# Three of eight samples' recurrent states moved from the attention heads into the last items of the in-projection

## The reference

```python
def step(h, inp):
    x_t, dt_t, da_t, b_t, c_t = inp
    h = jnp.exp(da_t)[..., None, None] * h + jnp.einsum('bgjp,bgn->bgjpn', x_t * dt_t[..., None], b_t)
    return h, jnp.einsum('bgjpn,bgn->bgjp', h, c_t)
```

## Time and profile before

| | |
|---|---|
| median of 3 runs | 593.87 us (593.57 to 593.93) |
| the profiled execution | 591.05 us, its span 589.3 us |
| busy in the span: PE, PEld, DVE, ACT, POOL | 531.9 (90%), 449.1 (76%), 384.9 (65%), 290.6 (49%), 77.7 (13%) us |
| 0 to 130 us: PE, DVE, ACT busy | 117.59, 91.11, 44.72 us |
| 130 to 313 us (items with page steps) | 181.53, 101.81, 89.02 us |
| 313 to 348 us (bridge) | 33.92, 21.23, 22.78 us |
| 470 to 481 us (end of the heads) | 0.22, 10.73, 2.52 us |
| 481 to 589.3 us (out-projection and tail) | 96.93, 77.97, 45.94 us |

### The profile page before, as it was taken

One profiled execution on the slowest core, in us unless ns is written; L12 is line 12 of the kernel. 1 busy time (PEld: TensorE's weight loads), 2 busy tenths in 40 slices (PEclk: granted clock), 3 DMA queues, 4 the chain that ended last, 5 costly groups with the idle time before them and its releaser, 6 DMA issues.

```text
span 589.3 us, 12342 instructions
## 1 busy us (share of the span) xinstructions
PE 531.9 (90%) x4726; PEld 449.1 (76%) x4726; DVE 384.9 (65%) x735; ACT 290.6 (49%) x624; POOL 77.7 (13%) x102
## 2 busy tenths in 40 slices
PE   4999998999999999999998999898787639999992
PEld 4899997998888888888885456566543339999992
DVE  5674987766555677445334753767677898795675
ACT  7333232143565554552614754877858645645320
POOL 2110000000000000000002412433431000210520
PEclk9999999999999999999999999888989959999997
DMA  8233032296889877788753342432470083669552
GB/s 333 108 143 97 30 97 86 71 315 222 255 268 283 265 256 250 239 309 289 246 191 97 93 133 82 110 81 60 148 256 19 6 303 115 223 202 367 188 157 72
DMA packets 55692, 104.12 MB, mean 177 GB/s; under 512 B 7193, under 2 KB 25986, under 8 KB 55378
## 3 DMA queue, kind: packets, MB, share of 16 engines
q1 hardware_dynamic: 55634, 103.33, 53.7%
HBM read 95.68 MB, written 7.73 MB: 175 GB/s over the span
## 4 chain that ended last, share of the span: by engine, by line
PE 76%; DVE 14%; ACT 6%; issue 3%; DMA 1%; POOL 0%; DVEq 0%; SPq 0%; ACTq 0%
PE pm L1488 18%; PE pm L1490 16%; PE pm L1489 16%; PE px L1571 4%; PE px L1587 3%; PE px L1760 3%; PE px L1758 3%; PE pm L1709 2%; ACT dec L723 1%; PE pm L1747 1%; DVE hring L1175 1%; PE px L1700 1%; PE px L1723 1%; DVE w_lo L880 1%; DVE xbc L1239 1%
## 5 line engine op out<-in xcount | busy, mean ns | idle before, releaser
L1488 PE MATMUL pm<-xw_hi,w_lo 128*128 128x260 f32 x544 | 162.3, 298 | 9.4 <-DVE w_lo L1007 8.3
L1489 PE MATMUL pm<-xw_lo,w_hi 128*128 128x260 f32 x544 | 154.4, 284 | 0.0
L1490 PE MATMUL pm<-xw_hi,w_hi 128*128 128x260 f32 x544 | 154.2, 283 | 0.0
L1488 PEld LDWEIGHTS pm<-xw_hi,w_lo 128*128 128x128 f32 x544 | 103.0, 189 | 24.6 <-issue 11.9
L553 ACT ACTIVATE w_hi<-w_raw 128x1024 fp32r<-128x1024 f32 (+1 forms) x70 | 72.0, 1035 | 83.0 <-PE pm L1490 76.7
L880 DVE TENSOR_TENSOR w_lo<-w_raw,w_hi 128x1024 fp32r<-128x1024 f32 (+1 forms) x70 | 85.9, 1236 | 29.0 <-ACT w_hi L553 29.0
L1489 PEld LDWEIGHTS pm<-xw_lo,w_hi 128*128 128x128 f32 x544 | 103.1, 190 | 0.2
L1490 PEld LDWEIGHTS pm<-xw_hi,w_hi 128*128 128x128 f32 x544 | 103.1, 189 | 0.0
L1488 PE MATMUL pm<-mix_hi,w_lo 128*128 128x260 f32 x256 | 73.7, 288 | 11.8 <-DVE mixlo_s L1233 11.3
L1490 PE MATMUL pm<-mix_hi,w_hi 128*128 128x260 f32 x256 | 73.2, 286 | 0.0
L1488 PEld LDWEIGHTS pm<-mix_hi,w_lo 128*128 128x128 f32 x256 | 49.2, 192 | 12.4 <-issue 12.1
(11 more groups left out here) (273 smaller groups left out, 1048.7 us busy)
## 6 DMA issues: line engine op xcount, KB each, us to landing
page<-in_cache SPq DMA_DIRECT2D x128, 288.0 KB, 3.6
w_raw<-in_w_in SPq DMA_DIRECT2D x34, 512.0 KB, 5.0
w_raw<-in_w_out SPq DMA_DIRECT2D x32, 512.0 KB, 4.7
dec<-ac_dram SPq DMA_DIRECT2D x16, 256.0 KB, 9.1
hring<-in_ssm_state SPq DMA_DIRECT2D x8, 512.0 KB, 6.5
o_ssms<-hring SPq DMA_DIRECT2D x8, 512.0 KB, 7.0
w_raw<-in_w_qb SPq DMA_DIRECT2D x6, 384.0 KB, 3.0
xraw<-in_xT SPq DMA_DIRECT2D x4, 520.0 KB, 6.4
```

Source lines behind the costliest of these rows:

```text
L1488: pe.matmul(out, wl, xh, start=start, stop=False)
L1489: pe.matmul(out, wh, xl, start=False, stop=False)
L1490: return pe.matmul(out, wh, xh, start=False, stop=stop)
```

## The change

Samples 0, 1 and 2 (quads 0 to 5) are updated and read out in items 33 to 38 (`EARLY_QUAD`), one quad at the end of each item on VectorE, by a new `early_dots` that takes the product in two pairs of rows, not one of four, since its scratch `prod_e` is half as wide. Their decays on ScalarE stand at the end of items 24, 25, 26, 27, 33 and 34 (`EARLY_DECAY`). Quads 6 to 9 take the places that are left in slots 5, 6 and 7; slots 1 to 4 hold none; the out-projection's quads stay.

For this, states 0 and 1 lie in the tiles of gates z 12 to 15, and VectorE waits for their stores before it evacuates items 36 and 38; state 2 lies where `u` is, and VectorE waits for its store before `state(2)` in the bridge. The samples' convolution moves from item 34 to item 27 and its SiLUs from item 36 to item 28. dxs is loaded in item 20 into `dxs_e` and its exponential taken in item 22, behind that item's SiLUs. The transpose, copy and store of B and C move to items 31 and 32. B and C of one group of one sample are broadcast for each early quad into one buffer `bc_e`, after the quad before is done. `dxs` and `ys` are copied at the end of the in-projection. SP's order follows: the loads of states 0 to 2, dxs, the conv state and the early broadcasts and stores stand among the weight and page loads, and the waits for early stores ahead of the first out-projection weights are gone.

```diff
+BC_STEP = [n for n in range(NSTEP) if SLOT[n][0] == 31][0] - 1
...
-SLOT_QUADS = {1: {3: 0}, 2: {3: 1}, 3: {3: 2}, 4: {3: 3}, 5: {3: 4, 4: 5}, 6: {3: 6, 4: 7}, 7: {1: 8, 3: 9}}
+NEARLY = 3
+EARLY_QUAD, EARLY_DECAY = {33 + n: n for n in range(2 * NEARLY)}, {24: 0, 25: 1, 26: 2, 27: 3, 33: 4, 34: 5}
+SLOT_QUADS = {5: {3: 6, 4: 7}, 6: {3: 8}, 7: {1: 9}}
...
-    hring = ([at("hring0", [P, 8, NS], F, G_ + 32768), at("hring1", [P, 8, NS], F, G_ + 20480)]
-             + [at(f"hring{b}", [P, 8, NS], F, A_ + 4096 * (b - 2)) for b in range(2, NB)])
+    hring = ([at(f"hring{b}", [P, 8, NS], F, off) for b, off in enumerate((B_ + 12 * TB, B_ + 14 * TB, H_ + TB))]
+             + [at(f"hring{b}", [P, 8, NS], F, A_ + 4096 * (b - NEARLY)) for b in range(NEARLY, NB)])
+    dxs_e = at("dxs_e", [P, 2, 8, NB], F, H_ + 3 * TB + 1024)
+    ys_e = at("ys_e", [P, 8, NEARLY], F, H_ + 3 * TB + 1536)
+    bc_t = at("bc_t", [32, P], F, H_ + 4 * TB + 1024)
+    prod_e = at("prod_e", [P, 2, NS], F, H_ + 4 * TB + 1024)
+    bc_e = at("bc_e", [P, 2, NS], F, H_ + 5 * TB + 1024)
...
-    stS = at("stS", [P, XT, 3, NB], F, H_ + TB)
+    stS = at("stS", [P, XT, 3, NB], F, B_ + 8 * TB)
...
+        def load_bc_e(n):
+
+            b, g = n // 2, n % 2
+            if n:
+                sp.wait_ge(v_dot, 4 * n)
+            sp.dma_start(bc_e, bc_dram.rearrange("(k g b) n -> b g k n", g=GR, b=NB)[b, g].partition_broadcast(P))\
+              .then_inc(s_bce, 16)
+
+        def store_early(b):
+            if b:
+                sp.wait_ge(s_hs0, 16 * b)
+            sp.wait_ge(v_h, 8 * b + 8)
+            sp.dma_start(a["o_ssms"][b], hring[b]).then_inc(s_hs0, 16)
...
-            if i == 31:
-                sp.wait_ge(a_silu, XT)
-                sp.dma_start(stS, a["conv_state"]).then_inc(s_sts, 16)
...
+            if i == 20:
+                sp.wait_ge(v_aux, X_QL)
+                sp.dma_start(stS, a["conv_state"]).then_inc(s_sts, 16)
+                sp.wait_ge(s_dsd, 16)
+                load_dxs()
+            if i in (21, 23):
+                load_state((i - 21) // 2)
+            if i == 32:
+                sp.wait_ge(a_silu, XT)
+                load_state(2)
+                sp.wait_ge(a_bct, 1)
+                sp.dma_start(bc_dram, bc_t).then_inc(s_bcd, 16)
+                sp.wait_ge(s_bcd, 16)
+            if i in EARLY_QUAD:
+                load_bc_e(EARLY_QUAD[i])
+            if i in (35, 37):
+                store_early((i - 35) // 2)
...
-        sp.wait_ge(s_dsd, 16)
-        load_dxs()
+        store_early(2)
...
-        sp.wait_ge(a_bct, 1)
-        sp.dma_start(bc_dram, u[1][0:32, 0:P]).then_inc(s_bcd, 16)
+        sp.wait_ge(p_pv, 2)
+        sp.wait_ge(v_dot, 8 * NEARLY)
...
-        load_state(0)
-        sp.wait_ge(p_st, 2 * NCH)
-        load_state(1)
-        sp.wait_ge(s_bcd, 16)
         sp.wait_ge(p_cb, 2)
-        load_bcs(0)
-        load_bcs(1)
+        load_bcs(3)
+        load_bcs(4)
...
-        load_state(2)
-        sp.wait_ge(s_ssm, 16)
-        for b in range(3, NB):
+        for b in range(NEARLY, NB):
             load_state(b)
-        load_bcs(2)
-        store_state(0)
-        store_state(1)
-        sp.wait_ge(s_hs0, 32)
-        sp.wait_ge(v_dot, 16)
...
-        load_bcs(3)
...
-        load_bcs(4)
         load_bcs(5)
...
             if i >= NIN + 20:
-                store_state(i - NIN - 18)
+                if i - NIN - 17 < NB:
+                    store_state(i - NIN - 17)
...
+        def state_decay(n, steps_):
+
+            b = n // 2
+            act.wait_ge(a_dx, 1)
+            act.wait_ge(s_hl[b], 16)
+            for t in range(4 * (n % 2), 4 * (n % 2) + 4):
+                act.activation(hring[b][:, t, :], hring[b][:, t, :], ACT.Copy, scale=steps_[:, 1, t, b:b + 1]).then_inc(a_h, 1)
...
+            if n == BC_STEP:
+                act.wait_ge(p_bct, 1)
+                act.activation(bc_t, px[0:32, 2, KVR:KVR + P], ACT.Copy).then_inc(a_bct, 1)
...
@@ -707,11 +742,16 @@
             if i in (ZT[7] + 1, ZT[11] + 1):
                 for t in range(4, 8) if i == ZT[7] + 1 else range(8, 12):
                     silu_z(t)
-                if i == ZT[11] + 1:
-                    act.wait_ge(v_cs, 1)
-                    act.wait_ge(g_last, XT)
-                    act.activation(xbc[:, 0:8, NT:TT], cvs[:, 0, 0:8], ACT.Silu).then_inc(a_cvs, 1)
-                    act.activation(cvs[:, 1], cvs[:, 0], ACT.Silu).then_inc(a_cvs, 1)
+            if i == 22:
+                act.wait_ge(s_dx, 64)
+                act.activation(dxs_e[:, 1], dxs_e[:, 1], ACT.Exp).then_inc(a_dx, 1)
+            if i == 28:
+                act.wait_ge(v_cs, 1)
+                act.wait_ge(g_last, XT)
+                act.activation(xbc[:, 0:8, NT:TT], cvs[:, 0, 0:8], ACT.Silu).then_inc(a_cvs, 1)
+                act.activation(cvs[:, 1], cvs[:, 0], ACT.Silu).then_inc(a_cvs, 1)
+            if i in EARLY_DECAY:
+                state_decay(EARLY_DECAY[i], dxs_e)
...
-        act.wait_ge(p_bct, 1)
-        act.activation(u[1][0:32, 0:P], px[0:32, 3, 0:P], ACT.Copy).then_inc(a_bct, 1)
...
-        act.wait_ge(s_dx, 64)
-        act.activation(dxs[:, 1], dxs[:, 1], ACT.Exp).then_inc(a_dx, 1)
...
+            if i in (ZT[12], ZT[14]):
+                dve.wait_ge(s_hs0, 16 if i == ZT[12] else 32)
...
+        def early_dots(n):
+
+            b, g = n // 2, n % 2
+            if n == 0:
+                dve.wait_ge(v_dx, 1)
+            dve.wait_ge(s_bce, 16 * (n + 1))
+            dve.wait_ge(a_h, 4 * n + 4)
+            for t in range(4 * g, 4 * g + 4):
+                dve.scalar_tensor_tensor(hring[b][:, t, :], bc_e[:, 0, :], dxs_e[:, 0, t, b:b + 1], hring[b][:, t, :],
+                                         ALU.mult, ALU.add).then_inc(v_h, 1)
+            dve.wait_ge(v_h, 4 * n + 4)
+            for k in range(2):
+                ts = slice(4 * g + 2 * k, 4 * g + 2 * k + 2)
+                if n or k:
+                    dve.wait_ge(v_dot, 4 * n + 2 * k)
+                link(dve.tensor_tensor(prod_e, hring[b][:, ts, :], bc_e[:, 1:2, :].to_broadcast([P, 2, NS]), ALU.mult))
+                dve.tensor_reduce(ys_e[:, ts, b:b + 1], prod_e, AX.X, ALU.add).then_inc(v_dot, 2)
...
-            if i == ZT[11] - 1:
+            if i == 27:
                 sample_conv()
+            if i == 29:
+                dve.wait_ge(a_cvs, 2)
+                dve.wait_ge(a_dx, 1)
+                dve.tensor_tensor(dxs_e[:, 0], xbc[:, 0:8, NT:TT], dxs_e[:, 0], ALU.mult).then_inc(v_dx, 1)
+            if i in EARLY_QUAD:
+                early_dots(EARLY_QUAD[i])
         sample_sum(NSTEP - 1)
         sample_out_t(1)
+        dve.tensor_copy(dxs, dxs_e).then_inc(v_dx, 1)
+        dve.tensor_copy(ys[:, :, 0:NEARLY], ys_e).then_inc(v_dx, 1)
...
+            if n == 2:
+                dve.wait_ge(s_hs0, 16 * NEARLY)
...
-            if n == 0:
-                dve.wait_ge(v_dx, 1)
-            dve.wait_ge(s_bcs[b % 2], 16 * (b // 2 + 1))
+            if n == 2 * NEARLY:
+                dve.wait_ge(v_dx, 3)
+            dve.wait_ge(s_bcs[b % 2], 16 * ((b - NEARLY) // 2 + 1))
...
-        dve.wait_ge(a_cvs, 2)
-        dve.wait_ge(a_dx, 1)
-        dve.tensor_tensor(dxs[:, 0], xbc[:, 0:8, NT:TT], dxs[:, 0], ALU.mult).then_inc(v_dx, 1)
...
+            if n == BC_STEP:
+                pe.wait_ge(a_cvs, 2)
+                pe.transpose(px[0:32, 2, KVR:KVR + P], cvs[:, 1, 8:12, :], cm[:, M_ID, :]).then_inc(p_bct, 1)
...
-        pe.wait_ge(a_cvs, 2)
         pe.wait_ge(v_cb, 2)
-        pe.transpose(px[0:32, 3, 0:P], cvs[:, 1, 8:12, :], cm[:, M_ID, :]).then_inc(p_bct, 1)
```

More of the change, by code:

```diff
@@ L726, in decays @@
             act.activation(dec[h % 6], dec[h % 6], ACT.Exp, scale=-1.0).then_inc(a_dec, 1)
-        def state_decay(n):
-            b = n // 2
-            act.wait_ge(s_hl[b], 16)
-            for t in range(4 * (n % 2), 4 * (n % 2) + 4):
-                act.activation(hring[b][:, t, :], hring[b][:, t, :], ACT.Copy, scale=dxs[:, 1, t, b:b + 1]).then_inc(a_h, 1)
         def gated_square(t):
@@ L830, in _ @@
                 for n in quads(s + 1, b):
-                    state_decay(n)
+                    state_decay(n, dxs)
             if 1 <= s <= 4:
```

30 lines of the change are left out of this document (13 added, 17 removed).

## The result

The changed kernel is slower: 604.70 us median of 4 runs (598.91 to 606.74) against 593.72 beside it on the same chip, ratio 1.018 (95% 1.013 to 1.022). The forecast was 591.5, its range ended at 596. The profiled execution took 605.37 us, its span (first instruction to last) is 603.3.

The account below looks back on a forecast made before the run. Four stages with different limits: TensorE nearly gapless except in the heads, where ScalarE's decays, then VectorE set the time. Gains of 8.8 us, less 5.5 in the in-projection and 1.0 in the bridge, gave -2.3: 591.5 us, range 587.5 to 596.

Parts of the forecast that it names:

- (d): In-projection, items 33 to 38: early quads wait for broadcasts landing in 4.9 us; costs 1.5 us, bounds 0 and 6.
- Rival 2: Early broadcasts land as slowly as the heads' bcs or worse, each early quad holding VectorE: 599 us; chance 0.12.
- SP's order: In-projection: dxs loads and the bc_dram wait ahead of weight and page loads cost 0, these being issued early enough.
- (a): In-projection, item 22: dxs exponential's table load comes ahead of ScalarE's copy of the probabilities; TensorE stands 0.8 us.
- (b): In-projection, items 24 and 26: ScalarE's state decays delay its copy of the probabilities, 0.5 us each, 1.0 together.
- (c): In-projection, item 27: sample_conv on VectorE delays the page sum, without slack; TensorE stands 2.2 us.
- The bridge: VectorE's third state step waits for the store of state 2, taken to land in 5.8 us; late by 1.0 us.
- The heads: Fewer quads on VectorE in the heads save 8.8 us: 2.1 and 1.6 at head 4, 5.1 in heads 6 and 7.
- Head 4's quad: Its removal moves the gate earlier, gain 2.1 us, and may keep TensorE's clock up, another 1.6 us.
- the end of the heads: Heads 6 and 7, path into the output projection: two quads of 2.57 us fewer on VectorE, gain 5.1 us.
- Slots 1 to 3: Heads 1 to 3: removing quads gains nothing, since they are off the path, which runs over ScalarE's decays.
- The sign: Whole kernel: change of -2.3 us; faster 0.59, same 0.19, slower 0.22.

Follow-up runs that it names:

- e6: Changed kernel, early quads' B and C read by a plain load of the same size from w_uk, not a broadcast (results of samples 0 to 2 wrong): 595.35 us.
- e10: Changed kernel run once more, unchanged, for a second trace: 602.95 us.
- e2: Changed kernel with the store of state 2 issued as soon as its last quad is done: 607.42 us.
- e7: Changed kernel with dxs exponential in item 23, decays in items 25, 27, 29, 31, dxs and conv state loaded one item earlier: 599.69 us.
- e5: Changed kernel with the edits of e7, e1 and e2, sample_conv on GpSimd, B and C transposed earlier: 606.04 us, ratio 1.021 to the kernel before.
- e4: Kernel before with only sample_conv moved to item 27, its state loaded in item 20: 595.39 us, ratio 1.004.
- e12: e8 with the store of state 2 again issued behind the whole in-projection and the decay loads: 587.78 us, ratio 0.994 to the kernel before.
- e8: e5 with SP's order mended: broadcasts wait for the quad before the last one, two state stores go ahead: 588.48 us, ratio 0.993 to the kernel before.
- e3: Changed kernel with the states of samples 0 to 2 left out everywhere: 590.86 us, ratio 0.998 to the kernel before.
- e1: Changed kernel with a second buffer for the early broadcasts, each issued one quad earlier: 597.22 us, ratio 1.011 to the kernel before.
- e9: e8 with the four quads of states 3 and 4 moved from heads 5 to 7 to heads 1 to 4: 583.10 us, ratio 0.984 to the kernel before.
- e11: Kernel before run once more, unchanged, for a second trace: 593.33 us.

## Why the prediction was wrong, step by step

*(d), the early quads: the step that failed.* "I take 4.9, below the 5.2 since the bytes are half." It is 6.9. The nearest row was the bcs' 6.7; halving the bytes took nothing off. A plain load of the same bytes took 4.4 (e6), so it was the broadcast that was slow, as far as e6's other source allows to say. The cost was put at 1.5 and bounded by 6; it was 14.8 us in the first trace, 8.8 in e10 and 8.9 in e2, where nothing that the quads wait for differs, 11.7 in e7. TensorE's four waits are 9.6 of it in the first trace and 8.1 in e10. Those behind the three odd quads, which the bound was for, are 7.2 in the first trace, 5.4 in e10 and 5.9 in e2. Two things were missing even in the bound: the first broadcast is late as well (item 33, 2.4 us), since SP issues it only after the store of bc_dram has landed, and these pauses can be followed by stretches at the lower clock: 5.1 us in the first trace, none in e10 or e2, whose clock in these items is 1.00. Rival 2 named this mechanism and its threshold, "about 7 us per landing", and came out at 599 with a chance of 0.12. The evidence in hand was for it: the one measured broadcast had that landing.

*SP's order, put at 0:* 0.8 to 3.2 in item 21. The forecast held that weights and pages are issued over one item before use. They are, but four dxs issues take 2.8 us of SP and the tiles behind them land late. e5 shows the same error at a higher price, 7.3 us of TensorE for one wait.

*(a), (b), (c):* 0.8, 1.34, 2.24 against 0.8, 1.0, 2.2. Right, each at its place, and e4 and e7 show them one by one. The Trainium skill's drain of 1.38 us for each table load (ScalarE: Activation LUTs, What ACT_TABLE_LOAD costs) would have made (a) 2.2; the wait is 0.75, so the trace decides against it here. The Trainium skill's 2.0 us plus bytes over 436 GB/s (DMA: Bandwidth & Descriptors, Anatomy of one DMA), fitted for another issue path, gives an estimated 2.3 us for the broadcast. That is a third of the 6.9; e6's plain load comes near it twice (2.4 and 2.5) and has a median of 4.4.

*The bridge:* the mechanism is right, the size isn't. TensorE is late by 2.56 us, not 1.0, and a lower clock behind it takes 1.8. The store landed in 6.2 us, not 5.8, and SP issued it 1.2 us later than the forecast had it: 346.99 less the 22.3 by which the bridge starts late is 324.7, not 323.43, since the ea loads ahead of it took 5.78 us and not 4.31. In the whole kernel this did not show: e2 gained nothing without it, and e12 and e8 do not differ, since the clock gave it back.

*The heads:* forecast 8.8, in e3, e1 and e2 8.7 to 8.8, in e8 and e5 9.4 and 9.6. That the sum meets the forecast is in part luck. Head 4's quad gives 4.5 (15.2 to 10.7; forecast 2.1 and 1.6 of clock, by the table 2.8 and 1.7), the end of the heads 5.5 (21.7 to 16.1; forecast 5.1), the stretch before it 0.3, and the clock in heads 2 to 5 takes 1.6 back. Slots 1 to 3 gave nothing: their stretches at full clock are 16 to 17.5 us with quads, without (e3), and with other quads (e9). The forecast said that it would be wrong if they shortened; in the first trace they did, from 19.4 and 18.5 to 16.8, and only the clock in it. The 14.5 of that trace is 8.8 and 5.7 of clock.

*The sign.* With 8.8 for the heads and the measured losses, the sum is -8.8 + 4.4 (a to c) + 1.1 (items 21 and 29) + 14.8 (d) + 4.4 (bridge) = 15.9 us. The clock in the heads takes 5.7 off, and the 2.1 at the start and the 1.8 at the end make it 14.0 of span, as measured. The 2.1 are the execution's, by e11. The 1.8 are the change's: the output projection takes 109.2 to 112.5 us in all eleven traces with states 0 to 2 out of the heads, and 107.7 to 107.8 in the three others. The forecast had no term for it, and no run took it apart.

## What to carry to other kernels

A transfer that is issued when its buffer comes free, and awaited by the next use, has only the time between the two uses to land in (here VectorE stood 13.7 us before four of six quads): price it at the landing of the nearest measured transfer of the same kind (a broadcast by a broadcast), and ask for a second buffer first. A wait on SP delays all that is queued behind it; in e5 SP's waits for quads 0 and 2, ahead of weights and of a store, cost 18.4 us with the lower clock behind them, more than all the early broadcasts in the changed kernel. Moving work into idle time can be free to the hundredth (the early quads in e8), if each piece stands where no one's result is behind it, and what is gained is then read from the stage that it leaves. Before a gain is put down to an edit, compare span times granted clock over all runs: e9's 5.4 us over e8 were mostly clock.
